# Experts' tokens gathered between the products, and eleven places for expert tiles

## The reference, cut to what matters

```python
combine = jnp.sum(jax.nn.one_hot(eid, N_EXPERTS) * gates[..., None], axis=1)
for e in range(N_EXPERTS):
    h = jax.nn.silu(t @ w_gate[e]) * (t @ w_up[e])
    y = y + combine[:, e:e + 1] * (h @ w_down[e])
```

## Time and profile before

| | us |
|---|---|
| median of 3 runs (1782.45 to 1792.45) | 1786.65 |
| the profiled execution | 1789.62 |
| its span, first to last instruction | 1788.3 |
| PE busy | 1627.2 (91%) |
| DVE busy | 919.6 (51%) |
| ACT busy | 674.8 (38%) |
| POOL busy | 541.6 (30%) |
| bytes moved | 444.78 MB, mean 249 GB/s |
| mean granted TensorE clock | 0.976 of 2.4 GHz |

### The profile page before, as it was taken

One profiled execution on the slowest core, in us unless ns is written; L12 is line 12 of the kernel. 1 busy time (PEld: TensorE's weight loads), 2 busy tenths in 40 slices (PEclk: granted clock), 3 DMA queues, 4 the chain that ended last, 5 costly groups with the idle time before them and its releaser, 6 DMA issues.

```text
span 1788.3 us, 22816 instructions
## 1 busy us (share of the span) xinstructions
PE 1627.2 (91%) x9313; PEld 1240.0 (69%) x9313; DVE 919.6 (51%) x1430; ACT 674.8 (38%) x989; POOL 541.6 (30%) x323
## 2 busy tenths in 40 slices
PE   6889989988889888879889999999999879999997
PEld 5767854334324333478788999999999767888886
DVE  5663432101001000266535379778733697888886
ACT  5553511001001000146535344444544795455453
POOL 3110100000000000121213154444455796777770
PEclk9988999999999999989899999999999999999999
DMA  7322569998998999843424355555566407999994
GB/s 266 118 95 71 189 247 376 393 421 350 420 422 347 422 421 421 316 150 118 153 95 149 134 176 195 182 181 198 187 212 213 147 1 256 354 353 341 351 347 161
DMA packets 99341, 444.78 MB, mean 249 GB/s; under 512 B 11152, under 2 KB 19856, under 8 KB 57632
## 3 DMA queue, kind: packets, MB, share of 16 engines
q1 hardware_dynamic: 85696, 403.85, 60.3%
q0 software_dynamic: 11264, 33.60, 5.1%
q10 hardware_dynamic: 2272, 5.82, 0.9%
HBM read 435.26 MB, written 7.86 MB: 248 GB/s over the span
## 4 chain that ended last, share of the span: by engine, by line
PE 74%; DMA 9%; ACT 8%; DVE 6%; issue 3%; POOL 0%; SPq 0%; ACTq 0%; DVEq 0%
PE ps L630 14%; PE ps L463 11%; PE ps L464 11%; PE ps L465 11%; PE ps L1037 10%; PE ps L1030 7%; DMA fix<-in_w_up 4%; PE ps L679 3%; DMA big<-in_w_up 3%; PE ps L651 2%; ACT y L2273 2%; DVE fix_parts L1068 1%; PE ps L593 1%; PE ps L616 1%; DMA fix<-in_w_in 1%
## 5 line engine op out<-in xcount | busy, mean ns | idle before, releaser
L465 PE MATMUL ps<-hh_parts,fix_parts 128*128 128x256 f32 x1152 | 327.2, 284 | 0.0
L630 PE MATMUL ps<-big 128*64 128x512 f32 x880 | 249.5, 601 | 31.4 <-DMA big<-in_w_up 13.2
L463 PE MATMUL ps<-hh_parts,fix_parts 128*128 128x256 f32 x768 | 219.3, 286 | 9.3 <-issue 5.6
L1068 DVE TENSOR_TENSOR fix_parts<-fix,fix_parts 128x1536 fp32r<-128x1536 f32 (+1 forms) x83 | 168.0, 2024 | 113.3 <-ACT fix_parts L1884 111.1
L465 PEld LDWEIGHTS ps<-hh_parts,fix_parts 128*128 128x128 f32 x1152 | 222.3, 193 | 0.0
L2313 POOL TENSOR_TENSOR fix_parts<-fix,fix_parts 128x512 fp32r<-128x512 f32 x58 | 139.0, 2398 | 261.6 <-ACT fix_parts L1884 261.6
L464 PE MATMUL ps<-hl_parts,fix_parts 128*128 128x256 f32 x768 | 217.8, 284 | 0.0
L630 PE MATMUL ps<-fix,big 128*64 128x512 f32 x656 | 197.4, 595 | 21.7 <-DMA fix<-in_w_up 7.6
L2313 POOL TENSOR_TENSOR big_parts<-big,fix_parts 128x512 fp32r<-128x512 f32 x12 | 23.7, 1975 | 548.3 <-ACT fix_parts L1884 548.3
L630 PEld LDWEIGHTS ps<-big 128*64 128x64 f32 x880 | 78.2, 138 | 155.9 <-issue 146.8
L1884 ACT ACTIVATE fix_parts<-fix 128x2048 fp32r<-128x2048 f32 x83 | 158.8, 1914 | 67.2 <-PE ps L1037 56.8
(11 more groups left out here) (393 smaller groups left out, 3633.5 us busy)
## 6 DMA issues: line engine op xcount, KB each, us to landing
fix<-in_expert_u SPq DMA_DIRECT2D x64, 1024.0 KB, 5.1
big<-in_w_down SPq DMA_DIRECT2D x38, 1024.0 KB, 11.1
fix<-in_expert_v SPq DMA_DIRECT2D x38, 1024.0 KB, 7.8
big<-in_w_gate SPq DMA_DIRECT2D x36, 1024.0 KB, 11.1
big<-in_w_up SPq DMA_DIRECT2D x36, 1024.0 KB, 9.8
fix<-in_w_gate SPq DMA_DIRECT2D x28, 1024.0 KB, 11.7
fix<-in_w_up SPq DMA_DIRECT2D x28, 1024.0 KB, 9.6
fix<-in_w_down SPq DMA_DIRECT2D x26, 1024.0 KB, 11.1
```

The source lines that it names most:

```text
L463: pe.matmul(o, l[0], r[0], start=first, stop=False)
L465: return pe.matmul(o, l[1], r[0], start=False, stop=last)
L630: ins = pe.matmul(m.PS[64 * i:64 * i + 64, bank, :], lhs(h * k_of // 2 + k, i), view(t.place[t.slot[x]])[:, k, c0:c0 + 512], start=(h + k ...
L1068: nc.vector.tensor_tensor(m.fr(x[:, 0:end]), x[:, 0:end], m.fr(hi[:, 0:end]).bitcast(F32), ALU.subtract).then_inc(s.lo_v, 1)
```

## The change

The gather is cut into smaller pieces and moved. It is now made for two pairs at a time (n = 0 to 7), and in four quarters x of two chunks each: the moving operand has 256 columns (four experts), and two chunks share one bank. The first gather (n = 0) runs in one piece before pair 0. After it, each pair g up to 13 does two quarters of gather `g // 2 + 1`, right after the scatter of the pair before. Quarters 0 and 2 are moved by VectorE, 1 and 3 by ScalarE, and TensorE waits for both before down, which uses the same banks. The two buffers `XGS` are half as large.

Gates are turned into bank 5 (the up bank), half after the transposes of pairs 2, 6, 10 and half after those of 3, 7, 11; TensorE waits before the next up for the copy. The first group's go into banks 2 and 3. The scatter leaves its fourth quarter until after the transposes. VectorE makes the masks of the next group in pairs 0, 4 and 8, after the copy of the hidden tile.

Expert tiles get eleven places. Places 9 and 10 lie where the gather buffers were cut (`ACTS`, 4096 to 8192), and the first load into them waits for the eighth mix of the attention. Places 11 and 12 are `FIX` 3 and 4, and open when the last split weights that used them are through. The upper halves of the first tiles after the stage wait for the last expert tile in their place.

```diff
+MOE_PLACES = (0, 1, 2, 3, 4, 5, 6, 9, 10, 11, 12)
-    m.XGS = [x.rearrange("p (g k s) -> p g k s", g=4, k=8) for x in two(0, 4096)]
+    m.XGS = [x.rearrange("p (g k s) -> p g k s", g=2, k=8) for x in two(0, 2048)]
-    four = [m.FIX[:, 3, :], m.FIX[:, 4, :], 5, 6]
+    four = [11, 12, 5, 6]
-        free = (3, 4) if i == last_tile else range(7) if moe else range(5)
+        free = (3, 4) if i == last_tile else MOE_PLACES if moe else range(5)
+    t.place += [m.ACTS[:, 4096:6144], m.ACTS[:, 6144:8192], m.FIX[:, 3, :], m.FIX[:, 4, :]]
...
+def gather_bank(n, x):
+    return 6 + x % 2 if n or x < 2 else x % 2
+def pe_gather(pe, m, s, n, x):
...
+    bank = gather_bank(n, x)
+    for k in (2 * x, 2 * x + 1):
         for b in range(2):
+            r = m.fr(m.SDS[n // 2 % 2][:, b, 4 * (n % 2):4 * (n % 2) + 4].rearrange("p e s -> p (e s)"))
+            for i, y in enumerate((m.XSH, m.Y)):
+                ins = pe.matmul(m.PS[:, bank, 256 * (k % 2):256 * (k % 2) + 256],
+                                m.fr(y[:, b, :].rearrange("p (c k) -> p k c", k=8)[:, k, :]), r,
                                 start=(b + i == 0), stop=(b + i == 2))
...
-    pe_gather(pe, m, s, 0)
+    for x in range(4):
+        pe_gather(pe, m, s, 0, x)
+    pe.wait_ge(s.over, 1)
...
-            pe_scatter(pe, m, s, g - 1)
+            pe_scatter(pe, m, s, g - 1, (0, 1, 2))
+        if g < 14:
+            for x in (2 * (g % 2), 2 * (g % 2) + 1):
+                pe_gather(pe, m, s, g // 2 + 1, x)
         pe.wait_ge(s.hmul, g + 1)
...
+        if g:
+            pe_scatter(pe, m, s, g - 1, (3,))
+        if g % 4 >= 2 and g < 12:
+            pe_turn_gates(pe, m, s, q + 1, g % 4 - 2)
+        if g < 14:
+            pe.wait_ge(s.g_v, g + 3)
+            pe.wait_ge(s.g_a, g + 3)
         pe.wait_ge(s.htb, g + 1)
...
-        if g % 4 == 1 and g < 12:
-            pe.wait_ge(s.yg_v, g + 1)
-            pe.wait_ge(s.yg_a, g + 1)
-            pe_gather(pe, m, s, q + 1)
-            pe_turn_gates(pe, m, s, q + 1)
...
+    elif t.slot[i] in (9, 10):
+        nc.sync.wait_ge(s.att_p, 8)
```

More of the change, by code:

```diff
@@ L110, in signals @@
     s.gains_t, s.gains = one("gains_turned"), one("gains")
-    s.land = [one(f"tile_landed{i}") for i in range(9)]
+    s.land = [one(f"tile_landed{i}") for i in range(13)]
     s.used, s.hi, s.lo_v, s.lo_g = one("tile_used"), one("tile_hi"), one("tile_lo_dve"), one("tile_lo_pool")
@@ L375, in weight_tiles @@
     last_tile, late = len(plan) - 1, len(split)
-    four = [m.FIX[:, 3, :], m.FIX[:, 4, :], 5, 6]
+    four = [11, 12, 5, 6]
     of_high = lambda n: four[(n if n < n_first else n - n_first) % 4]
     ends = list(range(len(plan)))
-    held = {x: [split[n] for n in range(n_first) if of_high(n) is x] for x in (5, 6)}
+    held = {x: [split[n] for n in range(n_first) if of_high(n) == x] for x in four}
+    opens = {9: first["w_vm0"], 10: first["w_vm0"]}
     slot = []
@@ L382, in weight_tiles @@
         moe = first["moe"] <= i < first["w_vm1"]
-        free = (3, 4) if i == last_tile else range(7) if moe else range(5)
-        end = lambda x: max([ends[k] for k in range(i) if slot[k] == x] + held.get(x, [])[-1:], default=-1)
+        free = (3, 4) if i == last_tile else MOE_PLACES if moe else range(5)
+        end = lambda x: max([ends[k] for k in range(i) if slot[k] == x] + held.get(x, [])[-1:], default=opens.get(x, -1))
         slot.append(min(free, key=end))
@@ L405, in weight_tiles @@
     where = [of_high(n) for n in range(late)]
-    t.high = [t.place[x] if isinstance(x, int) else x for x in where]
+    t.high = [t.place[x] for x in where]
     two = four[:2]
@@ L409, in weight_tiles @@
     for n in range(late):
-        same = [k for k in range(n) if where[k] is where[n]]
+        same = [k for k in range(n) if where[k] == where[n]]
         t.high_before.append(split[same[-1]] if same else None)
-        if same and same[-1] < n_first <= n and isinstance(where[n], int):
+        if same and same[-1] < n_first <= n:
             t.high_before[n] = max(k for k in range(len(plan) - 128) if slot[k] == where[n])
-    last = [max(n for n in range(late) if where[n] is x) for x in two]
+    last = [max(n for n in range(late) if where[n] == x) for x in two]
     ring = sorted((0, 1), key=lambda x: last[x])
-    t.high += [(xf, two[ring[0]], two[ring[1]])[(n - late) % 3] for n in range(late, t.n_split)]
+    t.high += [(xf, t.place[two[ring[0]]], t.place[two[ring[1]]])[(n - late) % 3] for n in range(late, t.n_split)]
     t.high_before += ["kept", split[last[ring[0]]], split[last[ring[1]]]] + [split[n - 3] for n in range(late + 3, t.n_split)]
@@ L618, in pe_mix, with pe_pair @@
     ins.then_inc(s.att_p, 1)
-def pe_pair(pe, m, s, t, tile, lhs, banks_of, view, k_of):
+def pe_pair(pe, m, s, t, tile, lhs, banks_of, view, k_of, gathered=None):
     for h in range(2):
+        if gathered is not None:
+            pe.wait_ge(s.g_v, 2 * gathered + h + 1)
+            pe.wait_ge(s.g_a, 2 * gathered + h + 1)
         two = (tile + 2 * h, tile + 2 * h + 1)
@@ L633, in pe_pair @@
         ins.then_inc(s.used, 4)
[L636 to L640, removed]
+def gather_bank(n, x):
+    return 6 + x % 2 if n or x < 2 else x % 2
+def pe_gather(pe, m, s, n, x):
+    if n == 0 and x == 0:
         pe.wait_ge(s.xs_lo, 1)
         pe.wait_ge(s.xs_lo_v, 1)
[L643 to L647, removed]
+    if n % 2 == 0 and x == 0:
+        pe.wait_ge(s.sd, n // 2 + 1)
+    bank = gather_bank(n, x)
+    for k in (2 * x, 2 * x + 1):
@@ L652, in pe_gather @@
                                 start=(b + i == 0), stop=(b + i == 2))
[L653 to L659, removed]
-    pe.wait_ge(s.dw, q + 1)
[L661 to L668, removed]
@@ L671, in pe_scatter @@
-def pe_scatter(pe, m, s, g):
-    pe.wait_ge(s.yg_v, g + 1)
-    pe.wait_ge(s.yg_a, g + 1)
[L674 to L682, removed]
+    ins.then_inc(s.g_mm, 1)
@@ new lines, in gate_bank, with pe_turn_gates, pe_scatter @@
+def gate_bank(q, c):
+    return 5 if q else 2 + c
+def pe_turn_gates(pe, m, s, q, c):
+    pe.wait_ge(s.dw, q + 1)
+    for g in (2 * c, 2 * c + 1):
+        for b in range(2):
+            ins = pe.transpose(m.PS[:, gate_bank(q, c), (g % 2) * 256 + b * P:(g % 2) * 256 + (b + 1) * P],
+                               m.DWS[q % 2][:, b, 2 * g:2 * g + 2, :].rearrange("p e s -> p (e s)"), m.ident)
+    ins.then_inc(s.dw_t, 1)
+def pe_scatter(pe, m, s, g, parts):
+    if 0 in parts:
+        pe.wait_ge(s.yg_v, g + 1)
+        pe.wait_ge(s.yg_a, g + 1)
+        if g % 4 == 0:
+            pe.wait_ge(s.sc_v, g // 4 + 1)
+            pe.wait_ge(s.sc_a, g // 4 + 1)
+    for x in parts:
+        b, half = x // 2, x % 2
+        ins = pe.matmul(m.PS[:, x, :], m.SCS[(g // 4) % 2][:, g % 4, b * P:(b + 1) * P],
+                        m.YG[g % 2][:, 512 * half:512 * half + 512], start=(g == 0), stop=(g == 15),
+                        skip_group_check=True)
+    if 3 in parts:
+        ins.then_inc(s.scat, 1)
@@ L811, in tensor_first @@
     pe.wait_ge(s.out_a, after["km1"][1])
-    pe_gather(pe, m, s, 0)
+    for x in range(4):
+        pe_gather(pe, m, s, 0, x)
+    pe.wait_ge(s.over, 1)
+    pe.matmul(m.PS[0:1, 5, 0:1], m.ovn, m.tri[:, 0, 127:128], start=True, stop=True).then_inc(s.over_n, 1)
     for g in range(16):
         q = g // 4
-        xg = m.XGS[q % 2]
-        lhs = lambda k, i: xg[:, g % 4, k, 64 * i:64 * i + 64]
+        xg = m.XGS[g // 2 % 2]
+        lhs = lambda k, i: xg[:, g % 2, k, 64 * i:64 * i + 64]
         tile = t.first["moe"] + 12 * g
-        if g % 4 == 0:
-            pe.wait_ge(s.g_v, 4 * q + 4)
-            pe.wait_ge(s.g_a, 4 * q + 4)
         if g:
             pe.wait_ge(s.htb, g)
-        pe_pair(pe, m, s, t, tile, lhs, [(4, 0)], by_k, 8)
+        pe_pair(pe, m, s, t, tile, lhs, [(4, 0)], by_k, 8, g // 2 if g % 2 == 0 else None)
         if g:
@@ L1425, in dve_router @@
     dve_slot_gates(nc, m, s, v, 0)
+    for x in (0, 2):
+        dve_gather(nc, m, s, t, 0, x)
     ve.wait_ge(s.over_n, 1)
@@ L1455, in dve_slot_gates, with dve_gather @@
     ve.tensor_tensor(dw[:, 1], m.fr(sd[:, 1]).bitcast(F32), slot_column(m.CB, 1, q), ALU.mult).then_inc(s.dw, 1)
[L1458 to L1466, removed]
+def dve_gather(nc, m, s, t, n, x):
+    if n >= 2 and x == 0:
+        nc.vector.wait_ge(s.used, t.used[t.first["moe"] + 12 * (2 * n - 3) + 7])
+    nc.vector.wait_ge(s.g_mm, 4 * n + x + 1)
+    for k in (2 * x, 2 * x + 1):
+        src = m.PS[:, gather_bank(n, x), 256 * (k % 2):256 * (k % 2) + 256].rearrange("p (g s) -> p g s", g=2)
+        ins = nc.vector.tensor_scalar(m.XGS[n % 2][:, :, k, :], src, m.g_ffn[:, k:k + 1], None, ALU.mult)
+    ins.then_inc(s.g_v, 1)
 def dve_turn_gates(nc, m, s, q):
@@ L2082, in scalar_first, with gathered @@
     ac.dma_start(kvkeep[:, 2048:3072], m.DS[:, 3072:4096]).then_inc(s.kv_kept, 16)
[L2084 to L2091, removed]
+    def gathered(n, x):
+        if n >= 2 and x == 1:
+            ac.wait_ge(s.used, t.used[f["moe"] + 12 * (2 * n - 3) + 7])
```

(15 more changed lines are left out.)

47 lines of the change are left out of this document (20 added, 27 removed).

## The result

The changed kernel takes 1758.42 us, median of 4 runs (1754.14 to 1759.63), beside 1785.84 us for the kernel before in the same comparison (4 runs, 1782.45 to 1792.45): ratio 0.9838, 95% interval 0.9805 to 0.9871, so 23 to 35 us. Forecast were 1750 and a range of 1743 to 1766. The profiled execution took 1758.41 us with a span of 1756.9; its own gain over the profiled one of before is 31.4 us, where 37.3 were forecast.

The account below looks back on a forecast made before the run. Transfers at their ceiling bound the experts' stage, with dips where gathers free no places. Gains of 9.9 (places), 1.1 (start), 25.6 (lost time) and 0.7 (tail) make 37.3 us: forecast 1750, range 1743 to 1766.

Parts of the forecast that it names:

- The narrow gather at 0.245 us: Each half-width gather matmul on TensorE costs 0.245 us, set by its stationary loads; first gather 8.0 us, as before.
- Up to down in 8.1 us: Within a pair, scatter, gather piece and transposes between up and down take 8.1 us, against 4.9 before.
- Evictions of 0.33 us: ScalarE's evictions of gather quarters take 0.33 us each and lie beside later quarters.
- The first released tile lands 5.1 us after issue: First release at 244.8 us; the twelfth expert tile, loaded into it, lands at 249.9.
- One tile late, by 0.8: The place freed by down 0 at 265.5 us gets its tile 0.8 us after the due 269.8.
- An unbroken stream of 176 tiles: After the first released tile, 176 expert tiles follow at 2.485 us each, from 249.9 to 687.3 us.
- Transfers bind at the end: At the end of the experts' stage transfers bind by 5 us over TensorE, which binds the first pairs.
- The gain from the dips: In the experts' stage, 25.6 of 26.4 us of lost transfer time would be won back.
- The first rival: TensorE becomes the bound of the experts' stage: gain 25 us, 1761.5; chance 0.20 shared with half-filled places.
- The narrow gather at 0.12: Half-width gather matmuls take 0.12 us, gate starts 4 us earlier, transfers bind throughout: gain 41, 1745.5; chance 0.12.
- The slower rival: Half-width gather matmuls take over 0.5 us, pairs 4.1 us longer: 14 us slower, 1801; chance 0.05.
- the one by which the places do not fill: SP's queue holds no more than the tiles now in flight, dips partly return: gain 24; chance 0.20 shared with TensorE bound.

Follow-up runs that it names:

- plain: Changed kernel with tokens stored chunk by chunk, so the gather's stationary operand has no step, eleven places: 1752.9 us, ratio 0.9805 to the kernel before.
- twice: Changed kernel with every matmul of the later gathers issued two times: one run of 1794.16 us.
- thirteen: Changed kernel with two more expert-tile places, in HH and HL: 1749.95 us, ratio 0.9783 to the kernel before.
- seven: Changed kernel's gathers inside the pairs, but with the seven places of the kernel before: 1791.97 us, ratio 1.0017 to the kernel before.
- seven_plain: Changed kernel with seven places and tokens stored chunk by chunk, so the gather's stationary operand has no step: 1762.68 us, ratio 0.9874 to the kernel before.
- nine: Kernel before, its gather left in one block, with two more places at FIX 3 and 4: 1772.62 us, ratio 0.9903.
- eleven: Kernel before, its gather left in one block, with four more places, in FIX 3 and 4, HH and HL: 1762.03 us, ratio 0.987.

## Why the prediction was right, and where its size was off

The mechanism was right: places and the gather's move together take the dips away, and transfers bind at the end. The size was 37.3 us against 31.4 between the traces (27.4 between the medians). Term by term, in the traces:

- **The narrow gather at 0.245 us: right.** Neighbours in the changed kernel start 0.24 apart:

```profile
375.75 0.41 PE L659 MATMUL ps<-big_parts 128*128 128x256 f32 x1
376.00 0.40 PE L659 MATMUL ps<-big_parts,y_parts 128*128 128x256 f32 x1
```

  *plain* shows the reason, which the prediction had only inferred from the earlier trace rows. The rule of the Trainium skill, *SBUF — State Buffer*, "Door 1: The DMA port swizzle", that accesses crossing to a new 16-byte line each time pay for it, agrees: 337 ns with the step and 192 without.
- **Gate 8.35 us after the first gather's start: 8.10**, right. **Up to down in 8.1 us: 7.95** (372.79 to 380.74). **TensorE's pair of 29.1: 28.9.** Right.
- **Evictions of 0.33 us: 0.47**, wrong by the row chosen, a plain copy:

```profile
L2108 ACT ACTIVATE big<-ps,small x32: 465/470/475, 241.0 to 646.8; 128x256 f32<-128x256 f32 x32
```

  It cost 0.85 us once, before the first down (263.72 in the chain), and was hidden in all later pairs, as said.
- **The first released tile lands 5.1 us after issue: 5.57.** It was issued here and landed at 254.09:

```profile
248.52 0.33 SPq L2410 DMA_DIRECT2D big<-in_w_down  x1
```

  0.5 us lost. The row of 5.1 is a median of another load.
- **One tile late, by 0.8: by 1.27.** It landed at 275.24, 6.4 us after this issue:

```profile
268.80 0.33 SPq L2410 DMA_DIRECT2D fix<-in_w_up  x1
```

  It was freed when forecast (down 0 starts 20.2 us after gate, 20.7 were forecast); only the landing was slower. 0.5 us lost.
- **An unbroken stream of 176 tiles:** two more tiles came late, by 1.40 at 279.1 us and by 1.44 at 506.8 (the pair of 31.2 in the chain); nothing in the prediction stood for them. 2.8 us lost. The kernel before has four such tiles away from its dips, late by 1.40, 1.16, 0.95 and 1.50 at 289.8, 355.5, 483.6 and 583.1 us. The prediction counted these 5.0 us among its 26.4 and took them for won.
- The sum of these: 0.5 + 0.5 + 2.8 - 0.25 = 3.5. The stage was forecast at 232.75 to 707.7 = 474.9 and took 478.3, 3.4 more. **This is the failed part of the sum:** the term of the transfers, 249.9 + 176 x 2.485 + 0.8, was mis-sized by 3.8, landings slower than the row of 5.1 and a stream with three breaks instead of one. Put as the prediction's gains: 25.6 us from tiles no longer late became 22.4, since late tiles add up to 26.5 us before (the four above, 2.67 at 273.5 us, and 4.91, 7.72 and 6.20 behind the three gathers) and to 4.1 after (1.27, 1.40 and 1.44).
- **The start itself** came 4.0 us later, together with the lower clock in the attention, and what follows the stage 1.5 earlier. 37.3 - 3.4 - 4.0 + 1.5 = 31.4.
- **Transfers bind at the end: right,** and TensorE binds the first pairs, up to 471 us. The margin was mis-sized: 13 us by *twice*, not 5. *thirteen*, where TensorE binds up to the 13th pair, shows that it is small even so.
- **The gain from the dips** had no owner in the prediction. By *seven* the move alone gives nothing: it turns 4.9 us between up and down into 8, and so puts a loss of 2 us into each of 14 pairs, 28 in all, where late tiles had cost 26.5. I had the 8 us in the prediction, but set them against eleven places only; against seven, by 5.1 us to landing, I expected 0.6 a pair. In *seven* tiles freed at 359.39 and 390.94 landed 6.2 and 6.9 us later. Four places are what pays, and the halving of `XGS` by the new gather makes room for two of them.

The first rival, TensorE the bound, holds for the first eight pairs and no longer. The narrow gather at 0.12 was the right price for another storage: 41 us were worked out for it, and *plain* lowers the stage by 38. The slower rival had no part. Nor had the one by which the places do not fill: eleven tiles had landed by 245.3 us, before the twelfth was issued at 248.52.

## What to carry to other kernels

Count for each place-holding stretch of the consumer how long it frees nothing, and set it beside what the buffers hold less one landing: well below that the stretch is free, and past it each us cost a us in every round, as *seven* and *seven_plain* show. It is an estimate, and a high one: seven places of 2.485 us less a landing of 6.2 to 6.9 are 10.5 to 11.2, where the measured cover was the 6.1 us and the half of 3.65 behind them, 9.8. Spreading a block of work over the rounds helps only if the rounds have that cover; otherwise it makes one large gap into many small ones, in *seven* with about the same sum (28 for 26.5 us). Where a matmul does not get cheaper with fewer columns, look at the load of its stationary operand, and at the step it is read with.

## What the runs showed of the hardware that I had not expected

- The granted clock between 264 and 266 us was 0.50 in the kernel before, 1.2 GHz of 2.4, as its row shows; in the changed kernel it is 1.00, 2.4 GHz:

```profile
264.00:266.00 2.00, 2.00 (x8) 0.52 (x6) 0.00 (x0) 0.00 (x0) 0.00 (x0) 0.50 1.03 430
```

  The old gather leaves TensorE idle for 3.38 us between the gates and the transposes of pair 0, and 0.79 after them; in the changed kernel the gather fills that time. Six halves behind it take 23.2 to 23.5 us at the start of *nine* and *eleven*, 20.82 after. All four profiled executions of the old gather have this stretch, none of the eight of the new one. The prediction counted the dip at 260 us as one of places; part of it was the clock. No run took the idle time away by itself.
- With nothing to two tiles ahead of it, a load of 1 MB landed 5.57 and 6.4 us after its issue in the changed kernel, and 6.2 and 6.9 after its place came free in *seven*, where loads of the small experts show 5.1. In the kernel before the seven expert tiles issued with nothing in flight took 4.9 to 6.4. One median does not price a landing.
- The two tiles late by 1.4 us land within 4 us of a fetch of instructions: in the changed kernel one packet of 16 KB from 504.1 to 505.2 us. The four of the kernel before lie likewise, and in both its traced executions the fetch beside each is the first one of 16 KB after a moment with no tile in flight (transfers came back with the tiles landed at 273.5, 319.5, 447.7 and 574.1 us); the fetches that follow leave no late tile. The one at 279.1 us in the changed kernel fits this, the one at 506.8 does not. The stage has some 16 such fetches in either kernel; what decides was not tried and stays open.
